# A decoder trunk on one core: the first products start as input and first matrices arrive in five parts

## Chip, cores and metric

The kernel runs on one NeuronCore of a Trainium2 chip. The metric is the device time of one execution in microseconds, here the median of three runs. A profiled execution was recorded beside them; its span runs from its first to its last instruction.

## What is computed

256 tokens of width 1024 pass through two layers. Each layer is a half-weighted SwiGLU feed-forward block (inner width 2816), a mixer, and a second feed-forward block, every one behind an RMS norm and added to the residual stream; a final RMS norm ends it. Layer 0's mixer is Mamba-2 SSD beside an RG-LRU, layer 1's is differential attention. Everything is float32. The change touches only the first feed-forward block:

```python
def rms_norm(x, w, eps=NORM_EPS):
    xf = x.astype(jnp.float32)
    y = xf * lax.rsqrt(jnp.mean(xf * xf, axis=-1, keepdims=True) + eps)
    return (y * w.astype(jnp.float32)).astype(x.dtype)

def swiglu(x, w_gate, w_up, w_down):
    return (jax.nn.silu(x @ w_gate) * (x @ w_up)) @ w_down

h = h + FFN_RES_SCALE * swiglu(rms_norm(h, norm_ff1[i]), ffn1_gate[i], ffn1_up[i], ffn1_down[i])
```

## The kernel before

**Layout.** Features lie on the 128 partitions, tokens along the free axis. x is `h`, 8 tiles of 128 x 256. A float32 product is made of three products of a faster format: each operand is rounded to a high half and the rest is kept as a low half. For weights `whi` and `wlo` are the halves, for x times the norm's weights `xn[:, d, 0]` and `xn[:, d, 1]`. High times both halves of x is one matmul of 512 columns (`multiply_wide`, L217), low times high one of 256 columns (L220). The division by the root of the token's mean square (`rb`, one number per token) comes after the products, since it is the same for all features.

**Blocks and pairs.** The weights come in blocks through a ring of 4 slots (`raw`, `whi`, `wlo`). In a feed-forward block's first part, block 2p holds 128 columns of gate and block 2p + 1 the same columns of up, each 8 tiles (512 KB); the two are pair p. There are 22 pairs, then 8 pairs of the down matrix with blocks of 11 tiles. For each block SP issues a DMA when the low half of the block four before is made (`load`, L174), ScalarE rounds it (`split_hi`, L185), VectorE subtracts (`split_lo`, L190), and TensorE does 8 + 8 matmuls.

**What follows a pair.** Pairs use two groups of PSUM banks in turn. ScalarE copies the part with x's low half (`corrections`, L505), VectorE adds both parts into `gu` (`merge`, L570), multiplies by `rb` (`normalize`, L574), ScalarE takes the silu (L510), VectorE multiplies (`product`, L579), ScalarE rounds the result (`hidden_hi`, L514), VectorE makes its low half (`hidden_lo`, L584). TensorE may start pair p only when pair p - 2 has been merged (`s_gu`). Every engine runs its program in order; all waits are on counting semaphores. The order on VectorE from pair 2 on is, for each pair: low half of its first block, merge of the pair two before, normalize, low half of its second block, product, hidden low half. ScalarE's is: high half, corrections, high half, silu, hidden high half.

**The begin.** SP issues x in four transfers of two tiles, the vectors `vec` (all norm weights) after the first of them, then blocks 0 to 3, the ones matrix, and blocks 4 to 7. TensorE first does 17 products with a tile of zeros (L1898), the last six of them waiting for tiles of x. ScalarE and VectorE make the halves of x (L297, L307), then those of blocks 0 and 1, the squares of x (`input_squares`, L314) and their sums (`input_sums`, L318 to L322), then blocks 2 and 3. Behind pair 0 TensorE sums the squares over the partitions (`token_sums`, L385), ScalarE takes the root (L422), VectorE the reciprocal (L426). Only then do ScalarE and VectorE go on with blocks 4 and the following and with the merge of pair 0.

Of the kernel before, what the change touches and what calls it, by code (L numbers as in the profile page):

```python
# [20 lines left out]
P = 128  # L21
D, T, FF = 1024, 256, 2816
DT, FT = D // P, FF // P
# [3 lines left out]
EPS = 1e-6  # L27

RING = 4
WARM = 11  # L30
KD = FT // 2
SLOT = KD * P


XBC, LW = 1536, 1024
# [39 lines left out]
def trunk(nc, a, out, phases=PHASES):  # L75
    ctx = ExitStack()
    with ctx:
# [3 lines left out]
        def sem(name):  # L81
            return ctx.enter_context(nc.semaphore(name))
# [30 lines left out]
        s_vec = sem("s_vec")  # L113
        s_ones = sem("s_ones")
        s_const = sem("s_const")
        s_x = [sem(f"s_x{i}") for i in range(4)]
        s_eps = sem("s_eps")
        s_raw = [sem(f"s_raw{i}") for i in range(RING)]
        s_whi = sem("s_whi")
        s_wlo = sem("s_wlo")  # L120
        s_blk = sem("s_blk")
# [51 lines left out]
                sp.wait_ge(s_wlo, b - RING + 1)  # L173
            sp.dma_start(tile_of(raw, s, k), src).then_inc(s_raw[s], 16)  # L174

        def load_x(sp, i):
            tiles = slice(2 * i, 2 * i + 2)
            sp.dma_start(h[:, tiles, :], a["xT"].rearrange("(d p) t -> p d t", p=P)[:, tiles, :]).then_inc(s_x[i], 16)

        def split_hi(act, b, s, k, turn, ring_full=True):  # L180
# [103 lines left out]
        def fresh(eng, n, d):  # L284

            if n == 0:
                eng.wait_ge(s_x[d // 2], 16)
            else:
                eng.wait_ge(s_h, DT * (n - 1) + d + 1)

# [22 lines left out]
        def input_squares(act, d):  # L313
            act.activation(xsq[:, d:d + 2, :], h[:, d:d + 2, :], ACT.Square).then_inc(s_xsq, 1)  # L314

        def input_sums(dve):
            dve.wait_ge(s_xsq, DT // 2)
            dve.tensor_tensor(xsq[:, 0:4, :], xsq[:, 0:4, :], xsq[:, 4:8, :], ALU.add).then_inc(s_xadd, 1)  # L318
            dve.wait_ge(s_xadd, 1)
            dve.tensor_tensor(xsq[:, 0:2, :], xsq[:, 0:2, :], xsq[:, 2:4, :], ALU.add).then_inc(s_xadd, 1)  # L320
            dve.wait_ge(s_xadd, 2)
            dve.tensor_tensor(sumsq[:], xsq[:, 0, :], xsq[:, 1, :], ALU.add).then_inc(s_xadd, 1)  # L322

        def squares_before(n):
            return n - 1
# [113 lines left out]
        def ffn_sync(sp, n, i):  # L439
            gate, up, down = ffn_matrices(i)  # L440
            b0 = 2 * first[n]

            def gate_up(it, ring_full):
                for s in range(RING):
                    c = it * (2 * P) + (s // 2) * P
                    load(sp, it * RING + (b0 + s), s,
                         (gate, up)[s % 2][:, bass.ds(c, P)].rearrange("(k p) m -> p k m", p=P), DT, ring_full)

            if n == 0:
                gate_up(0, False)  # L450
                sp.dma_start(con[:, 0:P], a["con"][:, 0:P]).then_inc(s_ones, 16)
                gate_up(1, True)
                sp.dma_start(con[:, P:NCON], a["con"][:, P:NCON]).then_inc(s_const, 16)
                sp.dma_start(heads[:], a["heads"]).then_inc(s_const, 16)
            with sp.Fori(2 if n == 0 else 0, FT // 2) as it:
                gate_up(it, True)
            with sp.Fori(0, DT // 2) as it:
                for s in range(RING):
                    rows = down[(s % 2) * KD * P:(s % 2 + 1) * KD * P, :]
                    load(sp, it * RING + (b0 + 2 * FT + s), s,  # L460
                         rows[:, bass.ds(it * (2 * P) + (s // 2) * P, P)].rearrange("(k p) m -> p k m", p=P), KD)

        def ffn_tensor(pe, n, i):
            p0, p1, hb = first[n], first[n] + FT, hidden_before(n)

            def gate_up(p, g, need=None, before_up=lambda: None):

                for m in range(2):
                    if m == 1:
                        before_up()  # L470
                    for part in early_tiles(n) if need and m == 0 else (None,):
                        multiply_wide(pe, p * 2 + m, 2 * g + m, DT, xn, 0, wide(g, m), need=need if m == 0 else None,
                                      part=part)

            def down(p, g, need=None):

                for m in range(2):
                    multiply_wide(pe, p * 2 + m, 2 * g + m, KD, hid, m * KD, wide(0, g), start=m == 0, stop=m == 1,
                                  need=need)

            if n:
                read_out(pe, p0 - 2)
            gate_up(p0, 0, lambda t: pe.wait_ge(s_xlo, DT * n + t + 1), lambda: read_out(pe, p0 - 1))
            token_sums(pe, n)
            gate_up(p0 + 1, 1)
            with pe.Fori(1, FT // 2) as it:
                for g in range(2):
                    pe.wait_ge(s_gu, it * 2 + (hb + g - 1))
                    gate_up(it * 2 + (p0 + g), g)
            read_out(pe, p1 - 2)  # L490
            down(p1, 0, lambda t: pe.wait_ge(s_hlo, hb + t + 1))
            down(p1 + 1, 1)
            with pe.Fori(1, DT // 2) as it:
                for g in range(2):
                    pe.wait_ge(s_h, it * 2 + (DT * n + g - 1))
                    down(it * 2 + (p1 + g), g)

        def ffn_scalar(act, n, i, before):
# [16 lines left out]
                               ACT.Copy).then_inc(s_hhi, 1)  # L515

            if n == 0:
                for d in range(DT):
                    residual_hi(act, 0, d)
                split_hi(act, 0, 0, DT, 0)  # L520
                input_squares(act, 0)
                split_hi(act, 1, 1, DT, 0)
                for d in (2, 4, 6):
                    input_squares(act, d)
                for b_ in (2, 3):
                    split_hi(act, b_, b_, DT, 0, False)
            else:
                begin_hi(act, p0, DT, before)
            token_rms(act, n)
            for it in range(1, FT // 2):  # L530
                for g in range(2):
                    for m in range(2):
                        split_hi(act, it * 4 + (2 * p0 + 2 * g + m), 2 * g + m, DT, it + t0)
                        if m == 0:
                            corrections(it * 2 + (p0 - 2 + g), g)
                    silu(it * 2 + (hb - 2 + g), g)
                    hidden_hi(it * 2 + (hb - 2 + g), g, it * 2 + (g - 2))
# [23 lines left out]
        def ffn_vector(dve, n, i, before):  # L561
# [31 lines left out]
                hidden_lo(q, g, it * 2 + (g - 2))  # L593

            if n == 0:
                for d in range(DT):
                    residual_lo(dve, 0, d)
                split_lo(dve, 0, 0, DT)
                split_lo(dve, 1, 1, DT)
                input_sums(dve)  # L600
                convert_lo(dve, p0 + 1, DT)
            else:
                begin_lo(dve, p0, DT, before)
            token_scale(dve, n)
            if n == 0:
                for g in range(2):
                    step(1, g, True)
            with dve.Fori(2 if n == 0 else 1, FT // 2) as it:
                for g in range(2):
                    step(it, g)  # L610
# [1266 lines left out]

        @block.sync
        def _(sp):
            load_x(sp, 0)  # L1880
            sp.dma_start(vec[:], a["vec"]).then_inc(s_vec, 16)
            for i in range(1, DT // 2):
                load_x(sp, i)
            for n, (kind, i) in enumerate(phases):
                {"ffn": ffn_sync, "hyb": hyb_sync, "att": att_sync}[kind](sp, n, i)
            for d in range(0, DT, 2):
                sp.wait_ge(s_fin, d // 2 + 1)
                sp.dma_start(out.rearrange("(d p) t -> p d t", p=P)[:, d:d + 2, :], fin[:, d:d + 2, :]
                             ).then_inc(s_out, 16)
            sp.wait_ge(s_out, 16 * DT // 2)  # L1890

        @block.tensor
        def _(pe):
            pe.wait_ge(s_warm, 1)
            for i in range(WARM + 6):
                if i >= WARM:
                    pe.wait_ge(s_xlo, i - WARM + 3)
                pe.matmul(banks[7][:, 0:T], rb[:, 0:P], rb[:], start=True, stop=True)  # L1898
            for n, (kind, i) in enumerate(phases):
                {"ffn": ffn_tensor, "hyb": hyb_tensor, "att": att_tensor}[kind](pe, n, i)  # L1900
            last_sums(pe)
            last_spread(pe)

        @block.scalar
        def _(act):
            act.wait_ge(s_eps, 1)
            act.activation(small[:, 0:1], eps[:, 0:1], ACT.Sqrt).then_inc(s_table, 1)
            act.wait_ge(s_vec, 16)
            before = []
            for n, (kind, i) in enumerate(phases):  # L1910
                before = {"ffn": ffn_scalar, "hyb": hyb_scalar, "att": att_scalar}[kind](act, n, i, before)
            nothing = lambda: None
            for left in before[:2]:
                left(nothing)
            last_square(act)
            for left in before[2:]:
                left(nothing)
            last_root(act)
# [93 lines left out]
```

## Time and profile before

| | us |
|---|---|
| median of 3 runs | 1064.26 (1063.46 to 1065.52) |
| profiled execution | 1063.65 |
| its span | 1061.9 |
| TensorE busy, matmuls | 1047.6 |
| VectorE busy | 795.6 |
| ScalarE busy | 612.4 |
| first product with weights | 10.77 after the span's start |

A busy time is the union of an engine's instructions, a share of it says little about a single stage. A timeline lists instructions in order of time, with neighbours of one kind merged: in such a line the second number is the length of the whole stretch and xN the count. In square brackets stands how long the engine had been idle and what ended that. TensorE's instructions overlap, so its pace is read from starts. A zero product, and the product with the ones matrix, leave two records each.

### The profile page before, as it was taken

How to read it: one execution, taken by the hardware profiler on the slowest of the kernel's cores; microseconds unless marked ns; L12 is line 12 of the kernel's file. 1: busy time of each engine (PE TensorE's matmuls, PEld its weight loads, DVE VectorE, ACT ScalarE, POOL GpSimd, SP SyncE). 2: the span in 40 equal slices, each digit the busy share in tenths (PEclk: the TensorE clock that was granted, in tenths of full speed). 3: DMA queues.
4: the chain of work that ended last, by engine and by line, in shares of the span. 5: the costliest groups of instructions: out<-in, count | busy, mean ns of one | idle time of the engine just before them, and what ended most of it. 6: DMA issues, size and time to landing. Idle time of an engine off the chain costs nothing.

```text
span 1061.9 us, 18438 instructions
## 1 busy us (share of the span) xinstructions
PE 1047.6 (99%) x6654; PEld 941.4 (89%) x6654; DVE 795.6 (75%) x1137; ACT 612.4 (58%) x980; POOL 51.1 (5%) x70
## 2 busy tenths in 40 slices
PE   9999999999998999999999999999999999999997
PEld 8888888899998988888888888888999998888886
DVE  6888776679869978887766888775699578888653
ACT  6555554468877555655435656543556765656541
POOL 0200012100000000000111000011100000000011
PEclk9999999999999999999999999999999999999999
DMA  8866776549644756666755666676566446667671
GB/s 246 217 195 189 217 201 165 157 122 270 168 115 124 214 145 196 197 189 198 218 156 164 191 192 198 188 218 170 155 158 164 120 128 202 190 193 209 186 199 40
DMA packets 369283, 190.14 MB, mean 179 GB/s; under 512 B 5920, under 2 KB 368704, under 8 KB 369232
## 3 DMA queue, kind: packets, MB, share of 16 engines
q1 hardware_dynamic: 368976, 188.89, 63.1%
q0 software_dynamic: 256, 0.59, 0.3%
q8 instruction: 29, 0.48, 0.2%
q14 instruction: 22, 0.18, 0.1%
HBM read 187.86 MB, written 1.07 MB: 178 GB/s over the span
## 4 chain that ended last, share of the span: by engine, by line
PE 93%; DVE 3%; ACT 2%; issue 1%; DMA 0%; DVEq 0%; ACTq 0%
PE psum L217 45%; PE psum L220 24%; PE psum L201 7%; PE psum L205 6%; PE psum L202 6%; DVE wlo L190 1%; PE psum L1898 1%; PE psum L1523 1%; DMA raw<-in_hyb_w_in 0%; DVE arena L1194 0%; ACT whi L185 0%; PE psum L953 0%; PE psum L880 0%; PE psum L936 0%; PE psum L954 0%
## 5 line engine op out<-in xcount | busy, mean ns | idle before, releaser
L190 DVE TENSOR_TENSOR wlo<-raw,whi 128x1024 fp32r<-128x1024 f32 (+1 forms) x324 | 416.9, 1306 | 75.3 <-ACT whi L185 74.0
L185 ACT ACTIVATE whi<-raw 128x1024 fp32r<-128x1024 f32 (+1 forms) x324 | 353.8, 1112 | 30.1 <-PE psum L205 23.2
L217 PE MATMUL psum<-xn,whi 128*128 128x512 f32 x1408 | 354.4, 393 | 0.5 <-DVE xn L307 0.5
L217 PEld LDWEIGHTS psum<-xn,whi 128*128 128x128 f32 x1408 | 253.5, 189 | 46.8 <-issue 0.6
L220 PEld LDWEIGHTS psum<-xn,wlo 128*128 128x128 f32 x1408 | 192.4, 190 | 13.8
L220 PE MATMUL psum<-xn,wlo 128*128 128x256 f32 x1408 | 196.9, 282 | 0.0
L217 PE MATMUL psum<-hid,whi 128*128 128x512 f32 x704 | 171.8, 391 | 0.0
L217 PEld LDWEIGHTS psum<-hid,whi 128*128 128x128 f32 x704 | 128.1, 189 | 24.1
L201 PE MATMUL psum<-xn,whi 128*128 128x256 f32 x480 | 120.8, 289 | 0.3 <-ACT whi L185 0.3
L202 PE MATMUL psum<-xn,whi 128*128 128x256 f32 x480 | 117.5, 283 | 0.0
L510 ACT ACTIVATE arena<-arena 128x256 f32<-128x256 f32 x88 | 36.8, 419 | 110.5 <-DVE arena L574 110.5
L220 PEld LDWEIGHTS psum<-hid,wlo 128*128 128x128 f32 x704 | 92.9, 191 | 4.9
L201 PEld LDWEIGHTS psum<-xn,whi 128*128 128x128 f32 x480 | 91.7, 191 | 3.8 <-issue 3.4
L220 PE MATMUL psum<-hid,wlo 128*128 128x256 f32 x704 | 94.4, 282 | 0.0
L202 PEld LDWEIGHTS psum<-xn,whi 128*128 128x128 f32 x480 | 91.8, 191 | 0.2
L514 ACT ACTIVATE hid<-arena 128x256 fp32r<-128x256 f32 x88 | 36.8, 418 | 88.7 <-DVE arena L579 88.7
L297 ACT ACTIVATE xn<-h,vec 128x256 fp32r<-128x256 f32 x48 | 23.6, 504 | 103.9 <-DVE h L644 97.5
L584 DVE TENSOR_TENSOR hid<-arena,hid 128x256 f32 (+1 forms) x88 | 37.4, 425 | 59.8 <-ACT hid L514 59.8
L205 PE MATMUL psum<-xn,wlo 128*128 128x256 f32 x480 | 67.7, 283 | 0.4 <-DVE wlo L190 0.4
L574 DVE TENSOR_TENSOR arena<-arena,rb 128x512 f32<-128x512 f32 x88 | 60.9, 692 | 3.1
L570 DVE TENSOR_TENSOR arena<-psum,arena 128x512 f32<-128x512 f32 x88 | 60.2, 684 | 3.7 <-ACT arena L505 3.7
L205 PEld LDWEIGHTS psum<-xn,wlo 128*128 128x128 f32 x480 | 62.0, 192 | 0.6 <-DVE wlo L190 0.6
(228 smaller groups left out, 876.6 us busy)
## 6 DMA issues: line engine op xcount, KB each, us to landing
raw<-in_ffn_gate SPq DMA_DIRECT2D x88, 512.0 KB, 3.9
raw<-in_ffn_up SPq DMA_DIRECT2D x88, 512.0 KB, 3.9
raw<-in_ffn_down SPq DMA_DIRECT2D x64, 704.0 KB, 4.6
raw<-in_hyb_w_in SPq DMA_DIRECT2D x36, 512.0 KB, 4.8
raw<-in_dif_w_qkv SPq DMA_DIRECT2D x24, 512.0 KB, 4.5
raw<-in_hyb_w_out SPq DMA_DIRECT2D x16, 512.0 KB, 4.6
raw<-in_dif_w_o SPq DMA_DIRECT2D x8, 512.0 KB, 4.2
hid<-cs_rows SPq DMA_DIRECT2D x4, 512.0 KB, 7.2
```

The costliest lines, as they stand in the source:

```text
L185: act.activation(whi[:, s, 0:k * P], raw[:, s, 0:k * P], ACT.Copy).then_inc(s_whi, 1)
L190: dve.tensor_tensor(wlo[:, s, 0:k * P], raw[:, s, 0:k * P], whi[:, s, 0:k * P].bitcast(F32), ALU.subtract).then_inc(s_wlo, 1)
L201: pe.matmul(acc, hi[:, j, :], x[:, t, 0, :], start=start and j == 0, stop=False)
L202: pe.matmul(acc, hi[:, j, :], x[:, t, 1, :], start=False, stop=False)
L205: mm = pe.matmul(acc, lo[:, j, :], x[:, k0 + j, 0, :], start=False, stop=stop and j == k - 1)
L217: pe.matmul(acc, hi[:, j, :], x[:, t, :, :], start=start and j == 0, stop=False)
L220: mm = pe.matmul(acc[:, T:2 * T], lo[:, j, :], x[:, k0 + j, 0, :], start=False, stop=stop and j == k - 1)
L510: act.activation(act_g[:, g, :], gu[:, g, 0, :], ACT.Silu).then_inc(s_silu, 1)
L514: act.activation(hid[:, bass.ds(j, 1), 0, :].rearrange("p a t -> p (a t)"), hu[:, g, :], ACT.Copy).then_inc(s_hhi, 1)
L570: dve.tensor_tensor(gu[:, g, :, :], wide_parts(g)[0], cor[:, g, :, :], ALU.add).then_inc(s_gu, 1)
L574: dve.tensor_tensor(gu[:, g, :, :], gu[:, g, :, :], rb2, ALU.mult).then_inc(s_gn, 1)
L584: dve.tensor_tensor(v[:, 1, :], hu[:, g, :], v[:, 0, :].bitcast(F32), ALU.subtract).then_inc(s_hlo, 1)
```

## The change

x, gate and up of the first pair come in five parts (tiles 0-1, 2-3, 4-5, 6, 7), each part being x's tiles and the same rows of both matrices, 15 transfers instead of 6. ScalarE and VectorE round and subtract gate and up of a part in one instruction, as soon as it has landed. TensorE does the products of a part for both matrices before the next part's. The zero products are five, none waiting for x. `vec` is issued from ScalarE's queue. `input_sums` is cut into its three steps, with other work of VectorE between them. Pairs 2 and 3 are taken out of TensorE's and ScalarE's loops: pairs 0 and 1 are copied and merged before the token scale exists, the token sums stand inside pair 2, behind block 4, and what needs the scale follows. The loops of TensorE and ScalarE begin at `it` = 2 in the first feed-forward block.

The core of the diff (new semaphores and the cut of `input_sums` are left out):

```diff
-WARM = 11
+WARM = 5
+PARTS = ((0, 2), (2, 4), (4, 6), (6, 7), (7, 8))
...
+SLOT_IN = DT * P
...
-        def load_x(sp, i):
-            tiles = slice(2 * i, 2 * i + 2)
+        LAST = len(PARTS) - 1
+        def part_of(buf, i):
+            k0, k1 = PARTS[i]
+            return buf[:, 0:2, k0 * P:k1 * P]
+        def load_part(sp, i, gate, up):
+            k0, k1 = PARTS[i]
+            for s, w in enumerate((gate, up)):
+                sp.dma_start(tile_of(raw, s, DT)[:, k0:k1, :], w[k0 * P:k1 * P, 0:P]
+                             .rearrange("(k p) m -> p k m", p=P)).then_inc(s_part[i] if i < LAST else s_raw[s], 16)
+        def part_hi(act, i):
+            if i < LAST:
+                act.wait_ge(s_part[i], 32)
+                act.activation(part_of(whi, i), part_of(raw, i), ACT.Copy).then_inc(s_phi, 1)
+            else:
+                act.wait_ge(s_raw[0], 16)
+                act.wait_ge(s_raw[1], 16)
+                act.activation(part_of(whi, i), part_of(raw, i), ACT.Copy).then_inc(s_whi, 2)
+        def part_lo(dve, i):
+            src, top = part_of(raw, i), part_of(whi, i).bitcast(F32)
+            if i < LAST:
+                dve.wait_ge(s_phi, i + 1)
+                dve.tensor_tensor(part_of(wlo, i), src, top, ALU.subtract).then_inc(s_plo, 1)
+            else:
+                dve.wait_ge(s_whi, 2)
+                dve.tensor_tensor(part_of(wlo, i), src, top, ALU.subtract).then_inc(s_wlo, 2)
+        def load_x(sp, i, k0, k1):
+            tiles = slice(k0, k1)
...
-                eng.wait_ge(s_x[d // 2], 16)
+                eng.wait_ge(s_x[max(i for i, (k0, _) in enumerate(PARTS) if k0 <= d)], 16)
...
-                gate_up(0, False)
+                for i, (k0, k1) in enumerate(PARTS):
+                    load_x(sp, i, k0, k1)
+                    load_part(sp, i, gate, up)
+                for s, w in ((2, gate), (3, up)):
+                    load(sp, s, s, w[:, P:2 * P].rearrange("(k p) m -> p k m", p=P), DT)
...
+            def first_pair():
+                hi, lo = (part.rearrange("p s (k m) -> p s k m", k=DT) for part in (whi[:, 0:2, 0:SLOT_IN], wlo[:, 0:2, 0:SLOT_IN]))
+                for i, (k0, k1) in enumerate(PARTS):
+                    tiles = range(k0, k1)
+                    pe.wait_ge(*((s_phi, i + 1) if i < LAST else (s_whi, 2)))
+                    for m in range(2):
+                        for t in tiles:
+                            pe.wait_ge(s_xlo, t + 1)
+                            pe.matmul(wide(0, m), hi[:, m, t, :], xn[:, t, :, :], start=t == 0, stop=False)
+                    pe.wait_ge(*((s_plo, i + 1) if i < LAST else (s_wlo, 2)))
+                    for m in range(2):
+                        for t in tiles:
+                            mm = pe.matmul(wide(0, m)[:, T:2 * T], lo[:, m, t, :], xn[:, t, 0, :], start=False, stop=t == DT - 1)
+                        if i == LAST:
+                            mm.then_inc(s_blk, 1)
...
-            gate_up(p0, 0, lambda t: pe.wait_ge(s_xlo, DT * n + t + 1), lambda: read_out(pe, p0 - 1))
-            token_sums(pe, n)
-            gate_up(p0 + 1, 1)
-            with pe.Fori(1, FT // 2) as it:
+                gate_up(p0, 0, lambda t: pe.wait_ge(s_xlo, DT * n + t + 1), lambda: read_out(pe, p0 - 1))
+                token_sums(pe, n)
+                gate_up(p0 + 1, 1)
+            else:
+                first_pair()
+                gate_up(p0 + 1, 1)
+                pe.wait_ge(s_gu, hb + 1)
+                gate_up(p0 + 2, 0, before_up=lambda: token_sums(pe, n))
+                pe.wait_ge(s_gu, hb + 2)
+                gate_up(p0 + 3, 1)
+            with pe.Fori(1 if n else 2, FT // 2) as it:
...
-                for d in range(DT):
-                    residual_hi(act, 0, d)
-                split_hi(act, 0, 0, DT, 0)
+                for i, (k0, k1) in enumerate(PARTS):
+                    for d in range(k0, k1):
+                        residual_hi(act, 0, d)
+                    part_hi(act, i)
+                split_hi(act, 2, 2, DT, 0)
...
-                split_hi(act, 1, 1, DT, 0)
-                for d in (2, 4, 6):
-                    input_squares(act, d)
-                for b_ in (2, 3):
-                    split_hi(act, b_, b_, DT, 0, False)
+                input_squares(act, 2)
+                split_hi(act, 3, 3, DT, 0)
+                corrections(p0, 0)
+                input_squares(act, 4)
+                input_squares(act, 6)
+                split_hi(act, 4, 0, DT, 1)
+                corrections(p0 + 1, 1)
+                split_hi(act, 5, 1, DT, 1)
+                split_hi(act, 6, 2, DT, 1)
+                token_rms(act, n)
+                silu(hb, 0)
+                hidden_hi(hb, 0, 0)
+                split_hi(act, 7, 3, DT, 1)
+                silu(hb + 1, 1)
+                hidden_hi(hb + 1, 1, 1)
...
-            token_rms(act, n)
-            for it in range(1, FT // 2):
+                token_rms(act, n)
+            for it in range(1 if n else 2, FT // 2):
...
-                for d in range(DT):
-                    residual_lo(dve, 0, d)
-                split_lo(dve, 0, 0, DT)
-                split_lo(dve, 1, 1, DT)
-                input_sums(dve)
-                convert_lo(dve, p0 + 1, DT)
+                for i, (k0, k1) in enumerate(PARTS):
+                    for d in range(k0, k1):
+                        residual_lo(dve, 0, d)
+                    part_lo(dve, i)
+                split_lo(dve, 2, 2, DT)
+                split_lo(dve, 3, 3, DT)
+                merge(p0, hb, 0, True)
+                input_sums(dve, 0)
+                split_lo(dve, 4, 0, DT)
+                input_sums(dve, 1)
+                input_sums(dve, 2)
+                merge(p0 + 1, hb + 1, 1, True)
+                split_lo(dve, 5, 1, DT)
+                token_scale(dve, n)
+                normalize(hb, 0)
+                split_lo(dve, 6, 2, DT)
+                product(hb, 0)
+                hidden_lo(hb, 0, 0)
+                normalize(hb + 1, 1)
+                split_lo(dve, 7, 3, DT)
+                product(hb + 1, 1)
+                hidden_lo(hb + 1, 1, 1)
...
-            token_scale(dve, n)
-            if n == 0:
-                for g in range(2):
-                    step(1, g, True)
+                token_scale(dve, n)
...
-            load_x(sp, 0)
-            sp.dma_start(vec[:], a["vec"]).then_inc(s_vec, 16)
-            for i in range(1, DT // 2):
-                load_x(sp, i)
...
-            for i in range(WARM + 6):
-                if i >= WARM:
-                    pe.wait_ge(s_xlo, i - WARM + 3)
+            for i in range(WARM):
...
+            act.dma_start(vec[:], a["vec"]).then_inc(s_vec, 16)
```

## Rows read from the trace of the kernel before

**Rows 1.** The page, busy time of each engine, share of the span and instructions.
```profile
PE 1047.6 (99%) x6654; PEld 941.4 (89%) x6654; DVE 795.6 (75%) x1137; ACT 612.4 (58%) x980; POOL 51.1 (5%) x70
```

**Rows 2.** Timeline of the first 24 us: start, us, engine, line, operation, tiles, count.
```profile
0.75 0.45 SPq L178 DMA_DIRECT2D h<-in_xT  x1
...
1.23 9.64 PE L1898 MATMUL psum<-rb 128*128 128x256 f32 x34 [1.23 <-DVE rb L1923]
...
4.39 3.16 SPq L174 DMA_DIRECT2D raw<-in_ffn_gate  x1
...
7.59 1.85 SPq L174 DMA_DIRECT2D raw<-in_ffn_up  x1
...
9.66 1.06 ACT L185 ACTIVATE whi<-raw 128x1024 fp32r<-128x1024 f32 x1 [1.52 <-DMA raw<-in_ffn_gate]
...
10.77 1.89 PE L217 MATMUL psum<-xn,whi 128*128 128x512 f32 x7
...
11.46 1.06 ACT L185 ACTIVATE whi<-raw 128x1024 fp32r<-128x1024 f32 x1 [0.22 <-DMA raw<-in_ffn_up]
...
16.58 0.70 PE L385 MATMUL psum<-sumsq,con 128*128 128x256 f32 x2
...
17.32 0.47 ACT L422 ACTIVATE rms<-psum,eps 128x256 f32<-128x256 f32 x1 [1.18 <-PE psum L385]
...
18.71 1.74 DVE L426 RECIPROCAL rb<-rms 128x256 f32<-128x256 f32 x1
```

**Rows 3.** Zero products (L1898) in two stretches: ns min/median/max, first and last start.
```profile
L1898 PE MATMUL psum<-rb x6: 634/634/634, 2.7 to 4.8; 128*128 128x256 f32 x6
...
L1898 PE MATMUL psum<-rb x11: 379/379/379, 6.8 to 9.0; 128*128 128x256 f32 x11
```

**Rows 4.** DMA issues at 4.39 and 7.59 us: count, size, us from issue to landing.
```profile
raw<-in_ffn_gate SPq DMA_DIRECT2D x1, 512.0 KB, 8.9
...
raw<-in_ffn_up SPq DMA_DIRECT2D x1, 512.0 KB, 7.5
```

**Rows 5.** Timeline from 26 to 39 us, all engines, around the start of pair 4.
```profile
27.82 0.69 DVE L574 TENSOR_TENSOR arena<-arena,rb 128x512 f32<-128x512 f32 x1
...
28.30 2.00 PE L217 MATMUL psum<-xn,whi 128*128 128x512 f32 x8
...
28.43 1.22 DVE L190 TENSOR_TENSOR wlo<-raw,whi 128x1024 fp32r<-128x1024 f32 x1
...
30.01 0.42 ACT L514 ACTIVATE hid<-arena 128x256 fp32r<-128x256 f32 x1 [1.05 <-DVE arena L579]
...
30.34 1.04 ACT L185 ACTIVATE whi<-raw 128x1024 fp32r<-128x1024 f32 x1
...
30.46 0.42 DVE L584 TENSOR_TENSOR hid<-arena,hid 128x256 fp32r<-128x256 f32 x1 [0.48 <-ACT hid L514]
...
31.41 1.23 DVE L190 TENSOR_TENSOR wlo<-raw,whi 128x1024 fp32r<-128x1024 f32 x1 [0.53 <-ACT whi L185]
...
32.55 0.69 DVE L570 TENSOR_TENSOR arena<-psum,arena 128x512 f32<-128x512 f32 x1
...
33.27 0.69 DVE L574 TENSOR_TENSOR arena<-arena,rb 128x512 f32<-128x512 f32 x1
...
33.88 2.00 PE L217 MATMUL psum<-xn,whi 128*128 128x512 f32 x8
```

**Rows 6.** Timeline at the end of the pairs, 118 to 150 us.
```profile
129.06 0.60 ACT L505 ACTIVATE arena<-psum 128x512 f32<-128x512 f32 x1 [0.23 <-PE psum L220]
...
138.28 2.68 PE L217 MATMUL psum<-hid,whi 128*128 128x512 f32 x11
...
139.89 0.43 DVE L584 TENSOR_TENSOR hid<-arena,hid 128x256 fp32r<-128x256 f32 x1 [0.48 <-ACT hid L514]
```

**Rows 7.** TensorE after an idle stretch, timeline and one window (busy, PEclk, DMA, GB/s).
```profile
331.98 0.35 PE L201 MATMUL psum<-hid,whi 128*128 128x256 f32 x1 [3.51 <-DVE hid L1332]
...
333.00:334.00 1.00, 0.77 (x3) 0.54 0.00 0
```

More of the change, by code:

```diff
@@ L115, in trunk @@
         s_const = sem("s_const")
-        s_x = [sem(f"s_x{i}") for i in range(4)]
+        s_x = [sem(f"s_x{i}") for i in range(len(PARTS))]
         s_eps = sem("s_eps")
         s_raw = [sem(f"s_raw{i}") for i in range(RING)]
+        s_part = [sem(f"s_part{i}") for i in range(len(PARTS) - 1)]
+        s_phi = sem("s_phi")
+        s_plo = sem("s_plo")
         s_whi = sem("s_whi")
@@ L314, in input_squares, with input_sums @@
             act.activation(xsq[:, d:d + 2, :], h[:, d:d + 2, :], ACT.Square).then_inc(s_xsq, 1)
[L316 to L322, printed above, removed]
+        def input_sums(dve, step):
+            if step == 0:
+                dve.wait_ge(s_xsq, DT // 2)
+                dve.tensor_tensor(xsq[:, 0:4, :], xsq[:, 0:4, :], xsq[:, 4:8, :], ALU.add).then_inc(s_xadd, 1)
+            elif step == 1:
+                dve.wait_ge(s_xadd, 1)
+                dve.tensor_tensor(xsq[:, 0:2, :], xsq[:, 0:2, :], xsq[:, 2:4, :], ALU.add).then_inc(s_xadd, 1)
+            else:
+                dve.wait_ge(s_xadd, 2)
+                dve.tensor_tensor(sumsq[:], xsq[:, 0, :], xsq[:, 1, :], ALU.add).then_inc(s_xadd, 1)
         def squares_before(n):
@@ L479, in down @@
                                   need=need)
+            def first_pair():
[13 more added lines that the diff above has]
+                            mm.then_inc(s_blk, 1)
             if n:
                 read_out(pe, p0 - 2)
-            gate_up(p0, 0, lambda t: pe.wait_ge(s_xlo, DT * n + t + 1), lambda: read_out(pe, p0 - 1))
-            token_sums(pe, n)
-            gate_up(p0 + 1, 1)
-            with pe.Fori(1, FT // 2) as it:
+                gate_up(p0, 0, lambda t: pe.wait_ge(s_xlo, DT * n + t + 1), lambda: read_out(pe, p0 - 1))
+                token_sums(pe, n)
+                gate_up(p0 + 1, 1)
+            else:
+                first_pair()
[5 more added lines that the diff above has]
+            with pe.Fori(1 if n else 2, FT // 2) as it:
                 for g in range(2):
```

## The prediction

> **What bounds the kernel now.** I first read the page's busy table: the profiled execution has a span of 1061.9 us and the matmul engine is busy for 1047.6 us of it [rows 1]. So a microsecond is gained only where TensorE does something that is not the model's work, or has nothing to do. The table of times says that this execution took 1063.65 us, 1.75 us more than its span and 0.61 us under the median of the runs, 1064.26. I work out a difference and add it to either.
>
> The second view is the timeline of the first 24 us. TensorE issues zero products from 1.23 us (34 matmul records) and its first real product at 10.77 us [rows 2]. The first 9.5 us are therefore what this change can attack, and nothing else in the program is touched. The first product waits for two things that end together: the zero products, and block 0's high half (9.66 + 1.06 = 10.72 us), for which ScalarE had waited for the gate columns. The up block lands at 11.46 us [rows 2].
>
> The third view is the other two engines around the pairs that follow [rows 5]. TensorE starts a block every 2.79 us ((33.88 - 28.30) / 2), a pair every 5.58. It may not start pair 4 (33.88) before VectorE has read pair 2 out of its banks (the merge, 32.55 + 0.69 = 33.24). The slack is only 0.64 us. The VectorE/ScalarE loop behind that merge turns once per pair in 5.45 us (normalize at 27.82 and again at 33.27, 0.72 after the merge at 32.55). So this loop is nearly as long as TensorE's own work, and a head start on TensorE alone is not kept: the merge of pair 2 must move as far. The reader is to see two clocks here, TensorE's and the loop's, 0.64 us apart.
>
> **The change part by part.** Call s the time at which TensorE starts block 2 (the first of the second pair).
>
> *The first pair in parts.* The bytes ahead of block 2 are the same as before (x, gate, up, vec), in other order, so the last part should land when up did, 11.46. The third part ends at 1.5 MB of x and weights, the same bytes that stood before gate's landing, 9.66. Its two tiles and both matrices are 512 columns to round (0.6 us, between 0.42 for 256 columns and 1.05 for 1024), so TensorE can start it at 10.3. Two tiles of both matrices are a quarter of a pair, 1.40 us, the single tiles 0.70 each, and the last is ready at 11.9 (0.42 for 256 columns) [rows 5]. Pair 0 ends at 10.3 + 2.8 = 13.1 instead of 16.58 [rows 2]. Smaller pieces cost ScalarE 3 x 0.6 + 2 x 0.42 = 2.6 us for 2 x 1.06, and VectorE about 0.5 us more; both engines wait for data there, so this is hidden.
>
> *Block 2.* It landed at 4.39 + 8.9 = 13.3 and block 3 at 7.59 + 7.5 = 15.1 [rows 2, 4], 1.8 us apart for 524,288 bytes, 291 GB/s. Nothing shortens this. SP has now 15 issues ahead of it instead of 7. The seven took 4.39 - 0.75 = 3.64 us, 0.52 each, so block 2's issue begins near 8.5; before, SP stood in that issue until 7.55 because the queue was full. The queue thus still has work when the issue comes, though with less in hand. I take the landing at 13.3 and so s = 13.3 + 1.06 + 0.05 = 14.4. The bounds: s cannot lie before pair 0's end, 13.1; if the landing keeps its distance of 5.75 us from the end of its own issue (now 9.0), it is 14.8 and s = 15.9. I stay near the low one, since data and not issuing paced the blocks. TensorE has 2.5 us on before's 16.93 (16.58 and 0.35 for the sums), and stands idle for 1.3 us before it.
>
> *Five zero products, vec on ScalarE's queue.* Five products are 10 records. Six of them start from 2.7 to 4.8 us, 0.42 apart and 634 ns long, eleven from 6.8 to 9.0, 0.22 apart and 379 ns long [rows 3]: by these durations TensorE ran at the lower of its two levels (1.2 GHz) until about 4.8 us and at 2.4 GHz after. Ten records end near 5.3, before the first part can be ready. So they cost nothing, and the twelve that are gone gained nothing by themselves. vec moves to an idle queue; x was waiting for it by a fraction of a microsecond, hidden now too.
>
> *Blocks 4 and 5.* Their loads wait for the low halves of blocks 0 and 1, now both at about 12.4, where before block 4's could go 0.4 us sooner and block 5's had to wait for 13.8 (11.46 + 1.06 + 1.23, the last by the low half at 31.41 [rows 5]). Blocks 2 and 3 keep the queue busy until 15, so block 4 lands at about 17.4 and block 5 at 19.2, for use at s + 5.58 = 20.0 and 23.1. Hidden. Behind SP's wait stand only these loads; loads 6 and 7 wait for low halves 2 and 3, 15.6 and 17.7, and land by 22.5, in time too.
>
> *Sums in the third pair.* Before, the ones product stood behind pair 0 (16.58), the root began 0.74 us later (17.32, 0.47 long), the reciprocal took 1.74 [rows 2]. Now it stands behind block 4, three blocks after s: 14.4 + 8.37 = 22.8. The tree of adds is done by then, about 21.7, since the squares are made by 18.0. The product costs TensorE 0.35 us, as before. Root 23.5 to 24.0, reciprocal 24.05 to 25.8, against 18.71 to 20.45 before. The scale is 5.3 us later, and nothing of pairs 0 and 1 can be normalized ahead of it.
>
> *What must follow it.* VectorE's order is then: normalize 0, low half 6, product 0, hidden 0, normalize 1, low half 7, product 1, hidden 1, low half 8, merge of pair 2. ScalarE's high halves 7 and 8 stand behind hidden 0 and 1. By the starts in [rows 5]: to normalize 0.04, to low half 6 0.61, from there to the hidden copy 1.58, to hidden low 0.45, to normalize 0.4, to low half 7 0.61, to the hidden copy 1.58, to high half 8 0.33, to low half 8 1.07, to the merge 1.14, its length 0.69. Together 8.5 us. The merge of pair 2 ends at 25.8 + 8.5 = 34.3, and with it pair 4 starts, at s + 19.9. TensorE by itself would be ready at s + 6 x 2.79 + 0.35 = 31.5. Its head start of 2.4 us is spent in waits: 0.7 us for high half 7 ahead of block 7 (29.4 for 28.7), and 2.1 us ahead of pair 4. Against 33.88 pair 4 starts 0.4 us LATER.
>
> *Later.* The loop's 5.45 us are under 5.58, so TensorE is never held again in these pairs, but VectorE is 0.6 us closer behind it than before. At the end of the pairs ScalarE's read-out waited 0.23 us for TensorE; that wait goes and about 0.4 us of lag stays. The last hidden tile was done at 139.89 + 0.43 = 140.32, and the down block that began at 138.28 wants it as its eleventh tile, 10 x 0.23 us later, 140.58 [rows 6]. Slack 0.26, so about 0.15 us more is lost. After that all engines move together. Sum: +0.4 + 0.15 = +0.55 us: span 1062.4, profiled 1064.2, median of runs 1064.8. With s at 13.1 it would be -0.7, with 15.9 +2.1: 1063.5 to 1066.3.
>
> **The rivals.** (A) *The head start survives*: the merge chain is not what holds pair 4, and TensorE keeps its 2.4 us: 1061.9. For it: before, the merges were always in time. Against: the reciprocal would have to end by 31.5 - 8.5 = 23.0, and it cannot begin before the sums, three blocks behind s; even at s = 13.1 it ends at 24.5.
>
> (B) *The clock falls in the new gaps*, slower. Before, TensorE stood idle for 3.51 us until 331.98, and about 1.5 us after it came back its granted clock fell, 0.54 in the microsecond from 333 [rows 7], and work there took twice as long for some 3.1 us, a loss of 1.6. The new gaps (1.3 us ahead of block 2, 0.7 and 2.1 ahead of block 7 and pair 4) are shorter, with dense work between them. It decides if a gap of 2.1 us is enough; then 1064.8 + 1.6 = 1066.4.
>
> (C) *Small transfers are slow.* If the 128 KB pieces moved at half of 291 GB/s, the 2.1 MB of the first pair would need 7.2 us more, s = 21.6, and nothing downstream gives it back: 1064.8 + 7.2 = 1072.0. Against: the queue is kept full and the rows of 512 bytes are as long as before. The Trainium skill (DMA: Bandwidth & Descriptors, section Bandwidth) has the rule "Batch DMAs to ≥1 MiB for ≥75% of peak", which speaks against this change; its figures are for transfers issued from GpSimd, and no row here shows a 128 KB one.
>
> (D) *Nothing moves*: the loop settles where it was, 1064.3.
>
> **How the numbers follow.** Own forecast 0.68, A 0.10, B 0.10, C 0.03, D 0.09. A measurement of this kernel tells a change from none at about 0.2%, 2.1 us. The forecast with its bounds and D lie within that nearly whole; A is beyond it on one side, C on the other, and B on its edge. That gives faster 0.11, same 0.76, slower 0.13. The range goes from A's edge to past B: 1062.0 to 1066.9. The likeliest case alone: 1063.5 to 1066.3.
>
> **What the profile after would show.** Right: ten zero-product records; the first real product at 6 to 7 us and pair 0 over near 13; block 2 near 14.4; reciprocal near 24; TensorE idle for about 2 us just ahead of pair 4 with VectorE's merge as releaser, and pair 4 near 34.3 (33.88 before). Wrong: pair 4 near 31.5 (A), a granted clock under 1.00 before 45 us (B), block 2 later than 16 (C). The largest doubts are s, which moves everything one to one, and the 8.5 us chain.

## The result: 0.15% slower, with the head start spent ahead of pair 4

| | us |
|---|---|
| kernel before, median of 20 runs | 1064.37 |
| changed kernel, median of 20 runs | 1065.85 |
| ratio | 1.0015, 95% interval 1.0009 to 1.002 |
| profiled execution of the changed kernel | 1065.87, span 1064.1 |

The ratio is clear of no change, and small. The time lies in the range and between the bounds of the likeliest case. The predicted median, 1064.8, was 1.05 us too low.

Timeline of the changed kernel, first 42 us:

```profile
1.23 4.05 PE L1984 MATMUL psum<-rb 128*128 128x256 f32 x10 [1.23 <-DVE rb L2010]
...
5.76 1.20 PE L533 MATMUL psum<-xn,whi 128*128 128x512 f32 x4 [0.48 <-ACT whi L197]
...
10.50 0.42 ACT L201 ACTIVATE whi<-raw 128x256 fp32r<-128x256 f32 x1
...
12.22 0.40 PE L537 MATMUL psum<-xn,wlo 128*128 128x256 f32 x2
...
13.05 1.06 ACT L221 ACTIVATE whi<-raw 128x1024 fp32r<-128x1024 f32 x1 [2.14 <-DMA raw<-in_ffn_gate]
...
14.16 2.11 PE L253 MATMUL psum<-xn,whi 128*128 128x512 f32 x8 [1.55 <-ACT whi L221]
...
22.65 0.59 PE L424 MATMUL psum<-sumsq,con 128*128 128x256 f32 x2
...
23.79 1.75 DVE L465 RECIPROCAL rb<-rms 128x256 f32<-128x256 f32 x1 [0.76 <-ACT rms L461]
...
29.19 2.12 PE L253 MATMUL psum<-xn,whi 128*128 128x512 f32 x8 [0.36 <-ACT whi L221]
...
33.31 0.68 DVE L649 TENSOR_TENSOR arena<-psum,arena 128x512 f32<-128x512 f32 x1
...
34.13 2.82 PE L253 MATMUL psum<-xn,whi 128*128 128x512 f32 x8 [1.87 <-DVE arena L649]
...
41.35 2.00 PE L253 MATMUL psum<-xn,whi 128*128 128x512 f32 x8
```

Real work starts at 5.76 us (10.77 in [rows 2]) and block 2 at 14.16, where the kernel before has it at 16.93:

```profile
16.93 2.21 PE L217 MATMUL psum<-xn,whi 128*128 128x512 f32 x8
```

Then the lead goes: TensorE waits 0.36 us for high half 7 ahead of 29.19, and 1.87 us ahead of pair 4 until VectorE's merge (33.31 + 0.68 = 33.99). Pair 4 starts at 34.13, where it started at 33.88 [rows 5]. Pair 5 should follow at 39.71, but it starts at 41.35. Its first eight products last 2.82 us for 2.00. The windows of that stretch (length, TensorE's busy time and products, granted clock, DMA share, GB/s) say why:

```profile
34.00:35.00 1.00, 0.87 (x4) 1.00 0.15 28
35.00:36.00 1.00, 1.00 (x5) 0.64 0.91 258
36.00:37.00 1.00, 1.00 (x5) 0.50 0.81 242
37.00:38.00 1.00, 1.00 (x6) 0.50 0.65 168
38.00:39.00 1.00, 1.00 (x6) 0.65 1.00 298
39.00:40.00 1.00, 1.00 (x6) 1.00 0.19 55
```

The granted clock went to the lower level about 1.2 us after TensorE had come back and stayed there for some 3.4 us; that is the 1.64 us lost. The first down block starts 0.25 + 1.64 = 1.9 us later, first the kernel before, then the changed one:

```profile
134.44 2.68 PE L217 MATMUL psum<-hid,whi 128*128 128x512 f32 x11
```

```profile
136.32 2.69 PE L253 MATMUL psum<-hid,whi 128*128 128x512 f32 x11
```

That is nearly all of the 2.2 us between the spans. The other 0.3 us come later, past 330 us, where both kernels have the idle stretch of 3.5 us of [rows 7]. The low stretch behind it is not equally long in each execution: 3.4 us in four of the twelve profiles of this document, the one of the kernel before among them, and 6.8 us in the other eight, the one of the changed kernel among them.

### The profile page after: what moved, and what is told of

Same layout as the page of the kernel before. It is cut to its first block, busy times and chain, and to the rows that moved or that the text cites. A ratio compares the mean times of both kernels' runs of the same rounds, so it can differ in the third digit from the quotient of the medians.

```text
span 1064.1 us, 18405 instructions
## 1 busy us (share of the span) xinstructions
PE 1045.5 (98%) x6630; PEld 939.3 (88%) x6630; DVE 795.7 (75%) x1140; ACT 613.1 (58%) x983; POOL 51.0 (5%) x70
## 4 chain that ended last, share of the span: by engine, by line
PE 91%; DVE 3%; ACT 3%; issue 1%; SPq 1%; DMA 0%; DVEq 0%; ACTq 0%
PE psum L253 45%; PE psum L256 23%; PE psum L237 7%; PE psum L241 6%; PE psum L238 6%; DVE wlo L226 1%; ACT whi L221 1%; PE psum L1615 1%; DMA raw<-in_ffn_gate 0%; SPq L191 0%; DVE arena L1286 0%; PE psum L1045 0%; PE psum L972 0%; PE psum L1028 0%; PE psum L1046 0%
```

## Experiments

Two theories stood to be tested. C: the chain from the token sums over the scale to the merge of pair 2 lets pair 4 in, 19.9 us behind block 2. G: the new idle stretch costs the clock. The kernel before ran beside each set: 1064.42 for the first four, 1064.55 for the next four, 1064.36 for the last two.

**1. The gap filled.** Behind `gate_up(p0 + 3, 1)`:

```diff
+for _ in range(8):
+    pe.matmul(banks[7][:, 0:2 * T], xn[:, 0, 0, 0:P], xn[:, 1, :, :], start=True, stop=True)
```

> The changed kernel with eight more products of 512 columns between pair 3 and pair 4, made of x's first tile and written to a bank that nothing reads, so that they fill TensorE's wait for the merge of pair 2 (32.0 to 34.1 us in the changed kernel's trace). Theory G (the changed kernel loses because the idle stretch ahead of pair 4 lets the granted clock fall, some 3.3 us at half rate): the clock stays at 1.00 up to 45 us, pair 4 still starts near 34.1, pair 5 near 39.7 instead of 41.35; the time falls by 1.6 us against the changed kernel, to within 0.5 us of the kernel before. Rival H (the clock falls for another reason than this gap, or costs nothing that lasts): the time stays 1.5 us above the kernel before.

Measured 1064.74, ratio 1.0006 (0.9997 to 1.0015), 0.9 to 1.1 us under the changed kernel, whose interval overlaps this one. In the timeline the filling replaces the wait, and pairs 4 and 5 are 5.69 us apart instead of 7.2:

```profile
32.31 2.00 PE L554 MATMUL psum<-xn 128*128 128x512 f32 x8
34.34 2.11 PE L253 MATMUL psum<-xn,whi 128*128 128x512 f32 x8
...
40.03 2.00 PE L253 MATMUL psum<-xn,whi 128*128 128x512 f32 x8
```

The clock held at 1.00 until the late stretch of [rows 7]. This one timeline proves little, since the changed kernel also has executions without a fall (experiment 8). The 11 runs say more: none has one of the two mean clocks that set the changed kernel apart in experiment 8. G is well supported; the gain of about 1 us instead of 1.6 fits a fall that is there in a part of the runs.

**2. A shorter scale**, in the first feed-forward block alone. It leaves out the division, so its output is not the model's and only its time counts:

```diff
-            dve.reciprocal(rb[:], rms[:]).then_inc(s_rb, 1)
+            if n == 0:
+                dve.tensor_copy(rb[:], rms[:]).then_inc(s_rb, 1)
+            else:
+                dve.reciprocal(rb[:], rms[:]).then_inc(s_rb, 1)
```

> The changed kernel with the reciprocal of the first token scale replaced by a copy (the first feed-forward block is multiplied by the root instead of divided by it), which is 1.3 us shorter on VectorE (0.4 for 1.75). Theory C (pair 4 is let in by the chain sums, root, scale, normalize, low halves 6 to 8, merge of pair 2, 8.5 us behind the scale): pair 4 starts 1.3 us earlier, near 32.8, the gap ahead of it shrinks to 0.7 us and the clock stays at 1.00; 1062.9, 1.4 us faster than before. Rival (TensorE's own start or the arrival of blocks holds pair 4): pair 4 stays near 34.1 and the time near 1065.9.

Measured 1063.52, ratio 0.9992 (0.9983 to 1.0001). Nothing was changed on TensorE, and pair 4 starts 18.51 us behind block 2 instead of 19.97:

```profile
14.40 2.11 PE L253 MATMUL psum<-xn,whi 128*128 128x512 f32 x8 [1.78 <-ACT whi L221]
...
24.02 0.29 DVE L466 COPY rb<-rms 128x256 f32<-128x256 f32 x1 [0.76 <-ACT rms L461]
...
32.91 2.11 PE L253 MATMUL psum<-xn,whi 128*128 128x512 f32 x8 [1.06 <-DVE arena L652]
```

C holds: the copy took 0.29 us where the reciprocal took 1.75, and pair 4, 9 us behind, moved by the same 1.46 us. The gap ahead of it was 1.06 us instead of the expected 0.7, and the 1062.9 was 0.6 us too low, which no run explains.

**3. Only the order.** The kernel before with the new order of blocks 2 to 7, sums inside pair 2 and the later loops; the begin is untouched. On TensorE:

```diff
-            token_sums(pe, n)
-            gate_up(p0 + 1, 1)
-            with pe.Fori(1, FT // 2) as it:
+            if n:
+                token_sums(pe, n)
+                gate_up(p0 + 1, 1)
+            else:
+                gate_up(p0 + 1, 1)
+                pe.wait_ge(s_gu, hb + 1)
+                gate_up(p0 + 2, 0, before_up=lambda: token_sums(pe, n))
+                pe.wait_ge(s_gu, hb + 2)
+                gate_up(p0 + 3, 1)
+            with pe.Fori(1 if n else 2, FT // 2) as it:
```

> The kernel before with the one part of the change that concerns order: pairs 0 and 1 merged ahead of the token scale, sums inside pair 2, the loops of TensorE and ScalarE from it = 2; x and the first blocks come as before, eleven and six zero products stay. Theory C: s (start of block 2) is 16.6, pair 4 starts 19.9 us later, at 36.5, against 33.88: 2.6 us slower, and with a fall of the clock in the gap 4.2, so 1066.9 to 1068.5. Rival (the order costs nothing, the loss is in the parts): 1064.3 or below.

Measured 1067.61 (5 runs), ratio 1.0036 (1.0022 to 1.005), inside the expected 1066.9 to 1068.5. Block 2 starts at 16.11, pair 4 at 35.97, 19.86 us later (19.97 in the changed kernel, 19.96 in experiment 1):

```profile
16.11 2.00 PE L217 MATMUL psum<-xn,whi 128*128 128x512 f32 x8
...
35.97 2.11 PE L217 MATMUL psum<-xn,whi 128*128 128x512 f32 x8 [1.87 <-DVE arena L588]
```

By itself the order costs 3.2 us in the median. Of these, 2.1 us are the later start of pair 4 (35.97 for 33.88). The profiled execution has no fall of the clock ahead of 330 us and took 1066.25, 1.8 us above the median of before; the slower runs were not profiled. The distance of 19.9 us is that of the order, whatever the begin.

**4. Only the parts.** Five parts, then the order of before, the sums behind block 2, all squares in ScalarE's wait for block 2. On TensorE, for the first feed-forward block:

```diff
 first_pair()
-gate_up(p0 + 1, 1)
-pe.wait_ge(s_gu, hb + 1)
-gate_up(p0 + 2, 0, before_up=lambda: token_sums(pe, n))
-pe.wait_ge(s_gu, hb + 2)
-gate_up(p0 + 3, 1)
+gate_up(p0 + 1, 1, before_up=lambda: token_sums(pe, n))
-with pe.Fori(1 if n else 2, FT // 2) as it:
+with pe.Fori(1, FT // 2) as it:
```

> The changed kernel's first pair in five parts, with the order of the kernel before behind it: sums inside pair 1 (behind block 2), scale next, then for each pair low half, merge, normalize, low half. ScalarE makes all squares while it waits for block 2, VectorE the first sum likewise. Theory C, by the same starts: reciprocal from 18.2 to 20.0, merge of pair 0 ends at 21.8, where pair 2 starts (22.71 before), pair 4 near 33.0, gaps of 1.7 us at most and the clock at 1.00: 0.9 us faster than before, 1063.5. Rival (the parts themselves cost what was lost): 1065 or more.

Measured 1064.15, ratio 1.0002 (0.9993 to 1.0011): between theory and rival. The profiled execution had pair 2 at 23.83 instead of 21.8, because here the clock fell behind the gap ahead of block 2 (windows as above):

```profile
14.00:15.00 1.00, 0.55 (x1) 0.74 1.17 291
15.00:16.00 1.00, 1.00 (x4) 0.50 0.92 251
```

The gap was 1.93 us, and the low level began as block 2 did, at 14.5. Three of its 11 runs show the mean clock of 0.993 that this one has, at 1065.3 to 1065.5; the others have 0.995 or 0.996 and a mean of 1064.0, where such runs of the kernel before have 1064.3. So even without a fall it seems only 0.3 us ahead: the parts and the early scale are worth little while the merges stand where they stood.

**5. A new order.** If VectorE's chain is the limit, its work has to go into its own waits. All squares are made while ScalarE waits for block 2, the sums follow behind block 2, root and reciprocal at once, and pairs 0 to 3 are written out with each merge moved ahead. TensorE has the sums in `before_up` of pair 1. VectorE's program behind the parts, in short (`lo(b)` is the low half of block b, a number in brackets the pair):

```
sums 0, lo(2), sums 1, sums 2, lo(3), merge(0), token_scale, lo(4), merge(1), normalize(0), lo(5), product(0), hidden_lo(0),
normalize(1), lo(6), merge(2), lo(7), product(1), hidden_lo(1), normalize(2), lo(8), merge(3), lo(9), product(2), hidden_lo(2),
normalize(3), lo(10), lo(11), product(3), hidden_lo(3), loop from it = 3
```

> The changed kernel's five parts with another order behind them: all squares of x while ScalarE waits for block 2, their sums in VectorE's waits, token sums behind block 2 (inside pair 1), root and reciprocal right after, and for pairs 0 to 3, taken out of the loops, each merge placed ahead of the normalize of the pair two before instead of after it. Theory C (VectorE's chain behind the scale decides): reciprocal from 18.4 to 20.2, pair 2 at 20.1, pair 4 at TensorE's own pace 17.1 us after block 2, near 31.4 (34.1 in the changed kernel), pair 6 between 42.6 and 43.3 (45.06 before); 1.8 us faster than before, 1062.6. Rival (the head start cannot be kept in any order, since VectorE's total work is the limit): pair 6 at 45 and 1064.4.

Measured 1062.02, ratio 0.9978 (0.9969 to 0.9987): 2.5 us faster than the kernel before and 0.6 us under the expectation, the best with experiment 10. Pair 4 starts 17.3 us behind block 2, at TensorE's pace, and pair 6 at 42.96 (45.06 before), with the merge it needs ending at 42.64. That is 2.1 of the 2.5 us:

```profile
14.49 2.11 PE L253 MATMUL psum<-xn,whi 128*128 128x512 f32 x8 [1.72 <-ACT whi L221]
...
31.79 2.00 PE L253 MATMUL psum<-xn,whi 128*128 128x512 f32 x8
...
42.96 2.00 PE L253 MATMUL psum<-xn,whi 128*128 128x512 f32 x8
```

```profile
18.60 1.74 DVE L465 RECIPROCAL rb<-rms 128x256 f32<-128x256 f32 x1
...
41.96 0.68 DVE L658 TENSOR_TENSOR arena<-psum,arena 128x512 f32<-128x512 f32 x1
```

**6. The new order, with seven products in the gap ahead of block 2.**

```diff
 first_pair()
+for _ in range(7):
+    pe.matmul(banks[7][:, 0:2 * T], xn[:, 0, 0, 0:P], xn[:, 1, :, :], start=True, stop=True)
```

> The same as the kernel with the new order, and seven more products of 512 columns between pair 0 and pair 1, made of x's first tiles and read by nothing, to fill TensorE's wait for block 2 (12.5 to 14.3 us). Theory G (an idle stretch here lets the clock fall in some runs): block 2 starts no later, the slowest runs go and the median falls by up to 0.5 us against the kernel without them, 1062.2. Rival (that wait never costs the clock): the same median within 0.3 us.

Measured 1062.45, ratio 0.9982 (0.9973 to 0.9991). Block 2 starts at 14.37. The median is 0.4 us above experiment 5, a little more than the rival's 0.3, with intervals that overlap: there is no gain. Here the wait of 1.7 us was seldom or never paid for, one run of experiment 5 in 11 having a mean clock under 0.995.

**7. No zero products**, `WARM = 0` in the changed kernel.

> The changed kernel without its five zero products. They end at 5.3 us and the first product with weights starts at 5.8, so they are in nobody's way. Theory G: TensorE's first work is then the parts; they run at the lower level (430 ns for a product of 512 columns instead of 216) until 9 us or later, pair 0 still ends before block 2 is there, since 5.6 us of work at half rate from 5.8 end near 14 at the latest if the rise comes by 10: no more than 0.5 us slower than the changed kernel. If the rise comes only after 14 us, block 2 starts late and the time is 1 to 3 us above the changed kernel's.

Measured 1065.03, ratio 1.0002 (0.9993 to 1.0011). It is not slower than the changed kernel (1065.68 beside it), and may be some tenths faster. By the lengths of its products (2.04 us for four of 512 columns, 1.20 otherwise) TensorE worked at the lower level until about 11.9 us, and pair 0 was done as block 2 came:

```profile
6.00 2.04 PE L533 MATMUL psum<-xn,whi 128*128 128x512 f32 x4 [6.00 <-DVE xn L343]
...
14.49 1.99 PE L253 MATMUL psum<-xn,whi 128*128 128x512 f32 x8
```

The slow level here is spent where TensorE would have waited.

**8. The changed kernel again.**

> The changed kernel itself, for a comparison on the same chip: 1.5 us above the kernel before. Theory G: its runs fall in two groups, those with a mean granted clock of 0.996 near the kernel before, those with 0.993 or less 1.5 us or more above it.

Measured 1065.68, ratio 1.0015 (1.0006 to 1.0024). This time the profiled execution had the same wait ahead of pair 4, but kept its clock, pair 6 came at 45.34 instead of about 46.9, and the span was 1062.0 instead of 1064.1:

```profile
14.10 2.11 PE L253 MATMUL psum<-xn,whi 128*128 128x512 f32 x8 [1.42 <-ACT whi L221]
...
34.07 2.11 PE L253 MATMUL psum<-xn,whi 128*128 128x512 f32 x8 [1.88 <-DVE arena L649]
...
45.34 2.00 PE L253 MATMUL psum<-xn,whi 128*128 128x512 f32 x8
...
134.73 2.68 PE L253 MATMUL psum<-hid,whi 128*128 128x512 f32 x11
...
138.56 2.70 PE L253 MATMUL psum<-hid,whi 128*128 128x512 f32 x11
...
140.18 0.43 DVE L663 TENSOR_TENSOR hid<-arena,hid 128x256 fp32r<-128x256 f32 x1 [0.48 <-ACT hid L581]
```

Each run also gives its mean granted clock. Of the 31 runs of the changed kernel, 19 have 0.994 or less, with a mean of 1066.3; 12 have 0.995 or more, with a mean of 1064.7. This difference of 1.6 us is not the fall alone: the kernel before has 14 runs of 81 at 0.993, 0.9 us slower than its others, without any new gap. The late low stretch moves the mean clock as well. The profiles with 0.996 have it 3.4 us long and those with 0.995 have it 6.8 us long. Experiment 7's profile has 0.993 without a fall ahead of pair 4.

Two values do set the kernels apart: 0.994 and 0.992 stand in 11 of the 31 runs and in none of the 81. How often the fall comes can only be estimated. The mean of the 31 runs is 1.3 us above the mean of the 81 (1065.7, 1064.4). If 0.3 to 0.5 us of that come without a fall (the down block here, 134.73 for 134.44; the runs with 0.996, 6 with a mean of 1064.1 for 21 with 1063.6), the rest is a fall of 1.64 us in half of the runs or a little more. What decides it is open: experiment 3, with the same wait, has 0.994 in two of its five runs, and experiment 7 has neither value in 11.

**9. Early merges with the late scale**: the changed kernel up to the reciprocal, the new order's merges behind it.

> The changed kernel up to the token scale (squares, sums and reciprocal where the change put them, near 24 us), and behind it the new order: the merges of pairs 2 and 3 ahead of low halves 7 and 9 instead of in the loop. It tells apart which half of the new order brought its gain. Theory C, by the same starts: pair 4 starts at TensorE's own pace or nearly, 31.9, but the merge of pair 4, which is back in the loop, comes 5.8 us after VectorE's own lag, near 44.3, so that pair 6 starts near 44.4 (42.96 in the new order, 45.06 before, 45.3 in the changed kernel without a fall of the clock): the merges alone bring 0.7 us against before, 1063.8. Rival (the early scale brought nothing, the merges all): 1062.0 as in the new order.

Measured 1064.18, ratio 1.0 (0.9991 to 1.0009), 0.4 us above the expectation. Pair 4 comes early, at 32.79 (0.9 us later than expected, with a wait of 0.63 us for low half 7 just ahead of it), and pair 6 at 44.79, let in by the merge that ends at 44.65:

```profile
32.79 2.00 PE L253 MATMUL psum<-xn,whi 128*128 128x512 f32 x8
...
43.97 0.68 DVE L660 TENSOR_TENSOR arena<-psum,arena 128x512 f32<-128x512 f32 x1
...
44.79 2.11 PE L253 MATMUL psum<-xn,whi 128*128 128x512 f32 x8 [0.35 <-DVE arena L660]
```

Moving merges alone hands the wait on by two pairs. With experiment 4, which has the early scale and the old place of the merges, this makes a table of four: against the kernel before, neither half (the early scale, the early merges) brings more than 0.3 us, both together (experiment 5) bring 2.5, and the changed kernel, with neither, loses 1.1 to 1.5.

**10. The new order without zero products.**

> The new order without the five zero products. TensorE then works at the lower level until about 12 us and ends pair 0 when block 2 is ready (in the changed kernel without them it did: 14.49 for 14.1 to 14.4), with no idle stretch ahead of block 2. Theory: the same time as the new order within 0.4 us, 1062.0 to 1062.4. Rival (the low level lasts longer in some runs and delays block 2): 1063 or more.

Measured 1061.80, ratio 0.9978 (0.9969 to 0.9987), the same as experiment 5 within what can be told. One expectation missed: an idle stretch of 0.93 us is left ahead of block 2. By the lengths of its products TensorE was at the lower level only until about 8.9 us here, 3 us less than in experiment 7:

```profile
8.57 1.36 PE L533 MATMUL psum<-xn,whi 128*128 128x512 f32 x4
...
14.14 2.11 PE L253 MATMUL psum<-xn,whi 128*128 128x512 f32 x8 [0.93 <-ACT whi L221]
```

It is the simpler of the two.

## Why the prediction was right, and what it mis-sized

- *Block 2 is paced by data.* Right: taken as 14.4, measured 14.16. The bytes ahead of it are the same, and fifteen issues took 0.5 us each, ending at 8.2, in time. The rule of the Trainium skill (DMA: Bandwidth & Descriptors, section Bandwidth) on large transfers did not decide here: with pieces of 256 to 64 KB the last was being rounded at 10.50, 1.0 us ahead of the 11.46 at which the up block's rounding began before. Pair 0 ended at 12.6, half a microsecond sooner than I had said. That the queue was full is my reading of one issue of 3.16 us, which no run tests.
- *The five zero products cost nothing*: right (experiment 7), and they bring nothing that can be measured (experiments 7 and 10).
- *The scale and the chain behind it.* Right: reciprocal at 23.79 for 24.05, merge of pair 2 ended at 33.99 for 34.3, pair 4 at 34.13. From the end of the reciprocal to the end of the merge it took 8.45 us for 8.5. Experiments 2, 3 and 5 show that the chain is the cause. Against the kernel before pair 4 started 0.25 us later for 0.4.
- *The step that was mis-sized is the clock*, my rival B. I gave it 1 chance in 10, its price 1.6 us, and left it out of the sum. It came in the profiled execution exactly there and for 1.64 us, with the sign that I had named for it, a clock under 1.00 before 45 us. In the runs it is worth 0.8 to 1.0 us on average, by the estimate of experiment 8. The sum without it, +0.55, stands beside +0.3 to +0.5. So the measured median lies between my case and B, and it was the width of the range that held it. The argument against B, that a wait of 2.1 us was shorter than the 3.51 us of [rows 7], was from one row and bounded nothing. I also misread that row: by its window of 0.54 the low level began about 1.1 us behind the return, not 1.5. And I left out the end of that trace, where TensorE waited 1.08 us ahead of 1054.38 and again 0.55, and the clock went low from 1056.7.
- *The last hidden tile* cost nothing where I had 0.15 us. In experiment 8's execution, without the fall, it was done at 140.61 and wanted at 138.56 + 10 x 0.23 = 140.86. The slack of 0.25 is that of before, so VectorE had made its lag good within the pairs.
- The bounds of s were wider than needed: 14.1 to 14.6 in all executions with parts.

## What to carry to other kernels

An earlier start of the busiest engine is kept only if the engine that frees its buffers starts earlier too. Here TensorE ran 5.58 us per pair and VectorE's loop 5.45, so there was nothing with which to catch up; before moving a start, follow the chain that releases the third or fourth unit of work. What does pay is to put the second engine's work into the stretches where it waits for the first data and to move the merges that free the banks ahead as well; here only both together paid. The wait that is left should be short, since a wait on TensorE can cost more than its length.

## What the hardware showed unexpectedly

The same wait of 1.9 us gave a fall of the granted clock in one execution of the same kernel and none in another (34.13 and 34.07 us, both with the merge as releaser). A wait of 1.93 us ahead of block 2 had one behind it in the profiled execution of experiment 4, and waits of 1.4 to 2.1 us in the profiled ones of experiments 1, 2, 3, 5, 7, 8 and 9 had none. So such an idle stretch cost nothing in one execution and about 1.6 us in another, no run shows what decides it, and a single profile can show either. Also, the clock column says 1.00 through the first 13 us in every trace, though the products of the kernel before last as long as at the lower level until 4.8 us, and those without zero products until about 11.9 us (experiment 7) or 8.9 (experiment 10): at a program's begin the length of a product tells the clock and the column does not.
